# Token-wise norms, another order beside the context units, a row-wise end and GpSimd residual adds in a two-block transformer kernel

## What is computed

```python
def rms_norm(x, w):                      # first block
    return x * lax.rsqrt(jnp.mean(x * x, axis=-1, keepdims=True) + EPS) * w

x = x + merged @ w_out                   # first out projection
u = jnp.square(jax.nn.relu(rms_norm(x, norm2_w) @ w_up))
...
def _modnorm(x, g_pre, shift, scale):    # second block
    return _rmsnorm(x, g_pre) * (1 + scale) + shift
def _residual(x, y, g_post, gate, weight):
    return x + weight * gate * _rmsnorm(y, g_post)
def _swiglu(h, w1, w3, w2):
    return (jax.nn.silu(h @ w1) * (h @ w3)) @ w2

x = _residual(x, _swiglu(_modnorm(x, g[0], m[0], m[1]), ...), g[1], m[2], 0.5)      # first SwiGLU
h_ctx = ...                                                                         # the same for 256 context tokens
# projections of _modnorm(x, ...) and _modnorm(h_ctx, ...), two attentions, merge:
x = _residual(x, _merge(...), g[3], m[5], 1.0)                                      # second out projection
x = _residual(x, _swiglu(_modnorm(x, g[4], m[6], m[7]), ...), g[5], m[8], 0.5)      # second SwiGLU, the result
```

## Time and profile before

| | us |
|---|---|
| median of three runs | 3106.71 |
| the profiled execution, its own time | 3113.06 |
| its span, first to last instruction | 3111.3 |
| PE busy / DVE busy / ACT busy / POOL busy | 2901.2 / 1552.6 / 1153.9 / 46.2 |
| granted TensorE clock, mean of the span | 0.960 of full speed |

### The profile page before, as it was taken

The page is one execution under the profiler, slowest core; times in us unless marked ns, Lnnn a source line. Parts: engine busy times, 40 slices in busy tenths (PEclk is TensorE's granted clock), DMA queues, the critical chain, the costliest instruction groups (busy, mean ns, idle before and its releaser), DMA issues.

```text
span 3111.3 us, 42874 instructions
## 1 busy us (share of the span) xinstructions
PE 2901.2 (93%) x14690; PEld 2367.9 (76%) x14690; DVE 1552.6 (50%) x2466; ACT 1153.9 (37%) x1768; POOL 46.2 (1%) x36
## 2 busy tenths in 40 slices
PE   8999999899998999999999999699889989599997
PEld 6878777689876888789988888577657777388885
DVE  3335444445655666567643844655443444533335
ACT  4333455432223232365532423522443443422222
POOL 0000000000000000000000000100000000000000
PEclk9999999899999999999999999888989999799998
DMA  3224211233433554446533333211111113133332
GB/s 114 67 74 135 62 41 53 73 117 118 133 122 95 169 161 142 142 135 179 167 108 95 95 95 92 76 41 40 44 33 31 31 48 96 42 94 93 95 94 68
DMA packets 504088, 288.65 MB, mean 93 GB/s; under 512 B 17577, under 2 KB 483962, under 8 KB 503850
## 3 DMA queue, kind: packets, MB, share of 16 engines
q1 hardware_dynamic: 503978, 287.25, 31.4%
HBM read 285.12 MB, written 2.10 MB: 92 GB/s over the span
## 4 chain that ended last, share of the span: by engine, by line
PE 67%; issue 20%; DVE 6%; ACT 4%; DVEq 1%; ACTq 1%; DMA 0%; POOL 0%; POOLq 0%; SPq 0%
PE unit_acc L776 61%; DVE w_lo L1958 2%; PE aux L1259 1%; ACT w_hi L1361 1%; PE aux L760 1%; PE aux L1235 1%; PE aux L1144 1%; PE aux L872 1%; PE aux L1126 1%; DVE mla_stat L2686 1%; DVE x L2453 1%; DVEq L2452 0%; ACT L1392 0%; PE aux L788 0%; PE aux L1127 0%
## 5 line engine op out<-in xcount | busy, mean ns | idle before, releaser
L776 PE MATMUL unit_acc<-h_hi,w_hi 128*128 128x512 f32 (+1 forms) x2376 | 839.0, 377 | 36.0 <-DVE w_lo L1958 17.2
L776 PE MATMUL unit_acc<-h_lo,w_hi 128*128 128x512 f32 (+1 forms) x2376 | 820.5, 370 | 0.0
L776 PE MATMUL unit_acc<-h_hi,w_lo 128*128 128x512 f32 (+1 forms) x2376 | 814.4, 367 | 0.0
L1958 DVE TENSOR_TENSOR w_lo<-raw,w_hi 128x1024 fp32r<-128x1024 f32 (+3 forms) x418 | 497.1, 1190 | 579.2 <-ACT w_hi L1361 571.8
L1361 ACT ACTIVATE w_hi<-raw 128x1024 fp32r<-128x1024 f32 (+3 forms) x418 | 430.3, 1030 | 699.6 <-PE unit_acc L776 649.6
L776 PEld LDWEIGHTS unit_acc<-h_hi,w_hi 128*128 128x128 f32 x2376 | 432.5, 192 | 140.2 <-issue 29.3
L776 PEld LDWEIGHTS unit_acc<-h_hi,w_lo 128*128 128x128 f32 x2376 | 432.3, 192 | 77.9
L776 PEld LDWEIGHTS unit_acc<-h_lo,w_hi 128*128 128x128 f32 x2376 | 433.5, 192 | 71.4
L776 PE MATMUL unit_acc<-branch_hi,w_hi 128*128 128x512 f32 x448 | 178.4, 398 | 0.0
L776 PE MATMUL unit_acc<-branch_lo,w_hi 128*128 128x512 f32 x448 | 176.8, 395 | 0.0
L776 PE MATMUL unit_acc<-branch_hi,w_lo 128*128 128x512 f32 x448 | 176.4, 394 | 0.0
(11 more groups left out here) (340 smaller groups left out, 3676.1 us busy)
## 6 DMA issues: line engine op xcount, KB each, us to landing
raw<-in_ffn_w_dram SPq DMA_DIRECT2D x180, 512.0 KB, 3.9
raw<-in_w_in_dram SPq DMA_DIRECT2D x142, 512.0 KB, 3.9
ada_raw<-in_w_ada_dram SPq DMA_DIRECT2D x72, 512.0 KB, 4.8
raw<-in_w_up_dram SPq DMA_DIRECT2D x32, 512.0 KB, 4.1
raw<-in_w_down_dram SPq DMA_DIRECT2D x32, 512.0 KB, 4.1
raw<-in_w_branch_dram SPq DMA_DIRECT2D x24, 512.0 KB, 4.2
raw<-in_ffn_w_dram SPq DMA_DIRECT2D x24, 384.0 KB, 3.4
raw<-in_w_out_dram SPq DMA_DIRECT2D x16, 512.0 KB, 4.1
```

Source lines behind the costliest of these rows:

```text
L776: last = pe.matmul(G[s][0:n, 512 * j:512 * j + m], w[:, k, 0:n], x[:, k, a:a + m], start=(k == 0 and i == 0), stop=(k == kc - 1 and i == 2))
L1958: dve.tensor_tensor(wl[s][:, 0:kc, :], raw[s][:, 0:kc, :], wh[s][:, 0:kc, :].bitcast(F32), ALU.subtract).then_inc(lo_split, 1)
```

## The change

It does five things.

1. **Token-wise norms.** In six of the norms over 1024 features (first out projection; two beside the context units; two of the second out projection; the one at the end) the sums, root and reciprocal are taken with tokens on partitions: PE multiplies each 128 x 128 block of squares, as stationary operand, by one column of ones (128 x 1 result, four blocks), ACT takes Sqrt of a 128 x 4 tile, DVE the reciprocal, and four transposes of the broadcast reciprocal put the row back on all partitions, in PSUM (`ROW`), where DVE reads it. The eighth chunk of squares is not added on DVE but accumulated by PE; for the norms of `X2` no chunk is added, PE accumulates all eight.
2. **Another order beside the context units.** Two of the eleven context units stand ahead of the residual, two within it, and seven after the second norm; DVE splits accordingly. GpSimd adds no squares any more.
3. **Second out projection.** ACT squares from the accumulator, ahead of the copy to `Y2`. DVE scales all chunks but adds only the even ones; GpSimd adds the odd ones (`x2_odd`).
4. **A row-wise end.** During the second SwiGLU PE transposes `X2` to rows (four groups of eight transposes, after its first four pairs of units) and ACT copies them to `x_tok`. In the last eight units ACT also writes `Y2` times the gain (`y_gain`), PE transposes two tiles of each chunk right behind the following unit, and at the end DVE makes each 128 x 1024 output tile in one operation, from PSUM, `tok_rstd` and `x_tok`, into four row buffers.
5. The loops over the last eight units of both SwiGLUs and over the second out projection are written out.

```diff
-        orow = [at(f"out_rows{s}", U2 + s * 4096, [D]) for s in range(2)]
+        orow = [at(f"out_rows{t}", U2 + t * 4096, [D]) for t in range(NT)]
+        xrow = [at(f"x_tok{t}", PH + 5 * ACT_B + t * 4096, [D]) for t in range(NT)]
+        YG = at("y_gain", EE, [KC, SEQ])
+        TOK = [t[:, 1016:1016 + NT] for t in (A[1], G[0])]
+        OUT = [A[0], A[1], G[1], G[0]]
+        ROW = [A[0][:, 512 * k:512 * k + SEQ] for k in range(2)]
 # PE
+            def token_matmuls(src, first, last, dst=TOK[0]):
+                for t in range(NT):
+                    done = pe.matmul(dst[:, t:t + 1], src[:, P * t:P * t + P], ones[:, 0:1],
+                                     start=(first and t == 0), stop=(last and t == NT - 1))
+                return done
+            def token_rows(k):
+                rows[0] += 1
+                pe.wait_ge(tok_rec, rows[0])
+                for t in range(NT):
+                    last = tr(ROW[k][:, P * t:P * t + P], tok_rstd[:, t:t + 1].to_broadcast([P, P]))
+                last.then_inc(tok_row, 1)
-            for k in range(NC):
+            def na_ctx(k):
                 unit(Count(U_NC + k), HCH, HCL, GC, n=QK if k == NC - 1 else P, ready=(ap_lo, 4 * KC))
-                if k in (0, 6):
-                    sum_squares(ss2, GS)
+            na_ctx(0)
+            token_sums_added(ss2, tm2)
+            token_rows(0)
+            na_ctx(1)
+            for c in range(KC):
+                token_sums(c, tm2)
+                if c in (2, 4):
+                    na_ctx(1 + c // 2)
+            token_rows(1)
+            for k in range(4, NC):
+                na_ctx(k)
...
-            sum_squares(ss2, GS)
-            sum_squares(ss2, GS)
+            token_sums_added(ss2, tm2)
+            token_rows(0)
+            for c in range(KC):
+                token_sums(c, tm2)
+            token_rows(1)
             swiglu(U_FB, 6 * KC + 8, 76)
-            sum_squares(ss2, GS)
+            token_sums_added(ss2, tm2, TOK[1])
+            y_rows(KC - 1)
 # ACT
+            def token_square(chunk, buf, n):
+                if toks[0] % KC >= 2:
+                    act.wait_ge(tok_used, toks[0] - 1)
+                act.activation(buf[toks[0] % 2][:, 0:n], chunk, ACT.Square).then_inc(tok_sq, 1)
+                toks[0] += 1
+            def token_root(src=TOK[0]):
+                act.drain()
+                act.wait_ge(tok_used, toks[0])
+                act.activation(tok_std[:, 0:NT], src, ACT.Sqrt, bias=eps_col, scale=1.0 / D).then_inc(tok_root, 1)
...
+                    if final:
+                        act.activation(YG[:, n, :], Y2[:, n, :], ACT.Copy, scale=resg[2][:, n, 0:1]).then_inc(o_yg, 1)
 # POOL
-            for c in range(KC):
-                pool.drain()
-                pool.wait_ge(nrm_sq, 7 * KC + c + 1)
-                ...
+            for c in range(1, KC, 2):
+                pool.wait_ge(y_scaled, c // 2 + 1)
+                pool.tensor_tensor(X2[:, c, :], X2[:, c, :], Y2[:, c, :], ALU.add).then_inc(x2_odd, 1)
+            pool.drain()
+            pool.wait_ge(x2_out, 2 * KC + KC // 2)
             pool.memset(Y2[:, :, :], 0.0).then_inc(y_zero, 1)
 # DVE
+            def token_rooted():
+                trows[0] += 1
+                dve.drain()
+                dve.wait_ge(tok_root, trows[0])
+                dve.reciprocal(tok_rstd[:, 0:NT], tok_std[:, 0:NT]).then_inc(tok_rec, 1)
+                dve.wait_ge(tok_row, trows[0])
-            split(Count(U_NC + 8))
-            rooted()
-            split(Count(U_NC + 9))
+            token_rooted()
+            split(Count(U_NC + 6))
...
-                dve.tensor_copy(orow[t % 2][:, :], A[t % 2][:, :]).then_inc(o_cp, 1)
+                dve.scalar_tensor_tensor(out=orow[t][:, :], in0=OUT[t][:, :], scalar=tok_rstd[:, t:t + 1],
+                                         in1=xrow[t][:, :], op0=ALU.mult, op1=ALU.add).then_inc(o_cp, 1)
```

More of the change, by code:

```diff
@@ L1074, in swiglu @@
                         sum_squares(ctx_sums[part], GC)
-                    with pe.Fori(1, 8) as n:
+                    n0 = 1
+                    if ctx_sums is None and part == 0:
+                        x_rows(0)
+                        n0 = NT
+                        for n in range(1, NT):
+                            up(part, n)
+                            x_rows(n)
+                    with pe.Fori(n0, 8) as n:
                         up(part, n)
@@ L1563, in _ @@
                 act.wait_ge(evicted[u.slot], val(u.turns() + 2))
-                square(X[:, n, META:T1], sqb, SEQ)
-            root(rstd, GS, D)
+                token_square(X[:, n, META:T1], sqb, SEQ)
+            token_root()
             for c in range(KC):
@@ L1666, in _ @@
                     modulate_chunk(0, 0, 0, s - 15, tm2[(s - 15) % 2][:, 0:SEQ], H2H)
-            def squares2(src, ready):
-                act.drain()
-                act.wait_ge(ap_lo, nap[0])
-                for c in range(KC):
-                    ready(c)
-                    square(src[:, c, :], tm2, SEQ)
             def swiglu(base, f0, final, chores=None):
@@ L2763, in _ @@
             mla_merge(Count(U_GATE + 2 * (KC - 1)), KC - 1, KC)
-            dve.memset(ss2[:, 0:SEQ], 0.0)
-            with dve.Fori(0, 4) as i:
-                for e in range(2):
-                    split(Count(U_OUT2 + 2 + e, (i, 2)))
-                    add_in_turn(ss2[:, 0:SEQ], tm2, SEQ, i, e)
-            nsq[0] += KC
-            rooted()
-            residual(1)
-            sums2()
+            for n in range(KC):
+                split(Count(U_OUT2 + 2 + n))
+                token_add(ss2[:, 0:SEQ], tm2, n)
+            token_rooted()
+            residual(1, ROW[0])
+            toks[0] += KC
+            token_rooted()
             normed()
```

219 lines of the change are left out of this document (120 added, 99 removed).

## The result

The changed kernel takes 3077.72 us, median of four runs (3074.64 to 3080.15); four runs of before taken with it have 3105.32 (3103.6 to 3107.78). The ratio of the times is 0.991, 95% interval 0.9893 to 0.9927. A second group of four runs of the changed kernel gave 3073.91 (3070.59 to 3075.71). Over all groups the medians are 3104.2 (42 runs of before, from 3098.87 to 3112.49) and 3075.2 (8 runs of the change): **29.0 us saved**, where 42.1 were forecast, and the first median lies 2.7 us above the top of the forecast range, 3075.

What follows compares the result with a forecast made beforehand. PE, busy 93% of the span, bounds the kernel except at four gaps; 17.0 + 4.2 + 12.5 + 13.5 - 5.1 = 42.1 us saved takes the median 3106.71 to 3064.6 us, range 3056 to 3075.

Steps and rivals of the forecast that it cites:

- The end: After the second SwiGLU: shorter norm chain and four wide DVE operations, program end at 3094.3 instead of 3111.3, 17.0 us saved.
- The second SwiGLU: PE-bound second SwiGLU: 32 transposes of X2 and 12 of y_gain at 0.117 us each, 5.1 us lost.
- Beside the context units: Around the residual and second norm there, bound by DVE's chain: earlier bias table, 12.5 us saved, 8 to 14.
- Step (a): Beside the context units: residual starts 4.3 us earlier, without Ln, second table load, Exp and a context unit's copy and split.
- Step (b): Beside the context units, residual: eight chunks at 1.43 and three splits, about 16 us against 22.9, 6.9 saved.
- Step (c): Beside the context units, last residual add to second scaling: 9.6 us against 11.4, 1.8 saved.
- Step (d): Beside the context units, modulation: same pace, but six chunks carry a split instead of three, minus 0.5 us.
- second scaling 13 us earlier: Expected sign beside the context units: the second norm's scaling starts 13 us earlier than before.
- The rival on the clock: Beside the context units: at half clock PE ends after 2020, that place gives nothing, time 3077; chance 0.10.
- The second out projection: Gap before the second SwiGLU: half clock at first, full for later chunks, 13.5 us saved, 10 to 17.
- the rival in which it and DVE disturb each other: Second out projection: GpSimd's odd adds slowed beside DVE, 8.9 us saved instead of 13.5, time 3069; chance 0.07.
- places 1 and 3: The program's end and the first out projection: by the profile page's table-load count each would save 1.28 us less.

Runs made afterwards that it cites:

- chunk_end: The changed kernel without its row-wise end: no transposes or y_gain in the second SwiGLU, token-wise norm kept, then residual chunks, transposes, copies; 3080.38 us.
- before_again: The kernel before, unchanged, run once more for a second trace; one run, 3100.05 us.

## Why the prediction was wrong

**The end (17.0 forecast).** From the SwiGLU's last matmul to the end 31.1 became 14.8 us: 16.3. The chain held step by step (scaling 3.9 us behind the last accumulator's start, forecast 4.0; four wide operations 4.85, forecast 5.0). What is missing is the time from the last operation to the end, 5.7 us and not the 4.56 taken from before.

**The second SwiGLU (-5.1).** 381.4 against 375.2: -6.2. The row-wise work cost 4.8 (381.4 less 376.7 in chunk_end), 0.108 us for each of the 44 transposes where 0.117 was forecast, and PE did not wait for it: it was busy for 331.47 of 331.47 us up to 3022.1 and for all 36.33 us behind that. The other 1.4 were no term of the sum: the 64-byte shift.

**The first out projection (4.2).** 11.52, 10.58, 10.57 became 6.93: 4.6 against the trace used, 3.6 against the others.

**Beside the context units (12.5), the step that failed.** What failed most is the step from an earlier bias table to an earlier end. The forecast took everything that DVE's chain gains as gained by the kernel; the attentions and the work behind them, where the change edits nothing, became 4 to 7 us longer. Of the 4.0 us that the first trace has more than before_again behind PE's restart, 3.9 are PE busy longer with the same matmuls: no wait, and the granted clock is all that the windows show to differ. The stage in front fell short as well. Step (a), the residual's start, held: 1941.8 is 9.2 us earlier, of which 5.3 came from upstream, so 3.9 against 4.3. Step (b) gave 4.7 instead of 6.9: the residual took 18.2 us, not 16. As written, eight chunks of 1.43 and three splits of 2.2 add up to 18.0; 16 comes out with two splits. Two stand there in the trace, and they took 2.65 and 4.05 us with their waits for context units that ran partly at half clock. Step (c) lost 1.0 instead of saving 1.8: it priced the sum at 0.94 and the context unit at 2.87 us, full clock, and 1.86 and 4.5 us were shown. Step (d) was about right (-1.2 for -0.5). Together the bias table began 6.4 us earlier than in the first trace of before, 7.6 to 8.2 than in the others, and it took 0.55 us longer. Net 2 to 3 us reached the end: some 10 of the 13 missing us.

Two numbers look like hits and are not. The sign "second scaling 13 us earlier" came out as 12.9, but 5.3 of these came from upstream. The rival on the clock has 3077, next to the measured 3077.72. It had PE end its units as late as before; in the trace PE was ready and idled 5.18 us for DVE's weights, and half clock did its harm ahead, in the units that DVE waited for, and behind, in the attention.

**The second out projection (13.5).** 38.1 (mean of three traces) became 26.9: 11.2, the forecast's own half-clock end. The residual's start and pace held: PE's sums begin 8.0 us behind the start of the last unit's last matmul, forecast 7.9. What failed is the clock. I had argued that it would come back after some 5 us of dense work, from the stretch 2710 to 2712. That work was wide matmuls; here 14.1 us of one-column passes left the clock at 0.50. The passes' price at half clock, 1.76 us a chunk, was exact (14.12 / 8 = 1.765). GpSimd was forecast to bring 1.4 us at most and brings nothing. The rule cited from the Trainium skill (GPSIMD Engine Reference, Engine selection), to leave such adds to VectorE, would have cost nothing: 26.47 against 26.9 us. GpSimd's four adds took 1.27 us each, so the rival in which it and DVE disturb each other did not occur.

**The sum.** 16.3 - 6.2 + 3.6 + 2.5 + 11.2 = 27.4 by the traces of the change against the other two traces of before; the medians say 29.0. **The table loads** behaved as the rows said: one is left at the root, so places 1 and 3 gained in full. **The slower rival** (PE waiting at the transposes) did not occur.

What stays open: why the clock falls where it does in the attention, and so why most of the earlier start is given back there, and why two traces of one kernel differ by 2.8 us in it; and by what way 64 bytes make a matmul longer.

## What to carry to other kernels

A start that is moved earlier is worth what arrives at the end, not what the stage in front gained: behind it may stand a stretch whose length depends on the granted clock, so compare several traces of the kernel before, and of the change, before a stage is credited. In a chain with short TensorE steps put operations that need nothing ahead of a split that waits for a unit, and price those steps at half clock. Small new tensors can move the large ones: here it paid to lay them over dead ones; putting them behind the large ones was not tried.

## What the hardware showed that was not expected

- PE busy with one-column matmuls stayed at the half clock: 13.94 of 14.20 us busy at 0.50. With one or two 512-column matmuls behind each sum (8 passes) the clock fell from 1.00 to 0.50 midway, with three it stayed at 1.00, in two kernels.
- The same matmuls of the neighbourhood attention took 232 to 244 us, by the clock granted (0.94 to 0.89). The length repeated within 0.1 us in four kernels that arrived 61.6 to 62.0 us behind the SwiGLU, but not in a fifth (237.6), and not in two traces of the changed kernel (235.05 and 237.82).
- 64 bytes of shift of the operands in SBUF made the second SwiGLU's matmuls 0.4% longer (375.2 became 376.7 us; taken out again, 381.4 became 380.0).
- DVE made a 128x1024 result from PSUM, a column and SBUF in 1.2 us (2.48 for two), no more than two copies of the same size took (2.46 in before).
